# Two gate stages of an encoder trunk, ordered row by row at their end

## What is computed

```python
def encoder_trunk(x, p, W):
    h = x
    for i in range(DEPTH):                      # 2
        hn = rmsnorm(h, W['norm_mix_g'][i])
        h = h + mixer(hn)                       # attention (i = 0), gated delta rule (i = 1)
        h = h + expert_choice_moe(rmsnorm(h, W['norm_ffn_g'][i]), ...)
        gate = jax.nn.sigmoid(rmsnorm(h, W['norm_ple_g'][i]) @ W['ple_w_gate'][i])
        h = h + (p[i] @ W['ple_w_proj'][i]) * gate
    return rmsnorm(h, W['final_norm_g'])
```

## Time and profile before

| what | us |
|---|---|
| median of three runs | 1686.21 |
| the three runs | 1686.21, 1686.31, 1683.01 |
| span of the profiled execution (its own time is not listed apart) | 1680.5 |
| busy: TensorE, its weight loads, VectorE, ScalarE, GpSimd | 1587.1, 819.3, 675.9, 439.1, 203.6 |
| mean granted TensorE clock | 0.987 of 2.4 GHz |

### The profile page before, as it was taken

One profiled execution on the slowest core, in us unless ns is written; L12 is line 12 of the kernel. 1 busy time (PEld: TensorE's weight loads), 2 busy tenths in 40 slices (PEclk: granted clock), 3 DMA queues, 4 the chain that ended last, 5 costly groups with the idle time before them and its releaser, 6 DMA issues.

```text
span 1680.5 us, 21275 instructions
## 1 busy us (share of the span) xinstructions
PE 1587.1 (94%) x8960; PEld 819.3 (49%) x8960; DVE 675.9 (40%) x1130; ACT 439.1 (26%) x972; POOL 203.6 (12%) x120
## 2 busy tenths in 40 slices
PE   8999899999989988899999999998999999899887
PEld 4464534343343324588875688844344433433243
DVE  3564411131210216889983477684111302102056
ACT  4232301101101103422125776534011010110043
POOL 2302000000000004352402211220000000000031
PEclk9999999999999999999999999999999999999999
DMA  8104699999999995012121110276999999999941
GB/s 288 77 18 183 276 423 421 428 427 429 428 424 427 427 421 212 1 51 102 50 101 51 27 27 2 102 300 250 392 426 428 428 427 428 423 428 426 426 167 50
DMA packets 54045, 454.56 MB, mean 270 GB/s; under 512 B 5187, under 2 KB 7519, under 8 KB 28991
## 3 DMA queue, kind: packets, MB, share of 16 engines
q1 hardware_dynamic: 53424, 452.90, 65.6%
q0 software_dynamic: 288, 0.22, 0.0%
q10 hardware_dynamic: 239, 0.09, 0.0%
HBM read 451.07 MB, written 2.13 MB: 270 GB/s over the span
## 4 chain that ended last, share of the span: by engine, by line
PE 70%; DVE 12%; DMA 8%; ACT 6%; issue 3%; ACTq 0%; SPq 0%; DVEq 0%
PE banks L2154 34%; PE banks L1499 12%; DMA ring<-in_moe_w_down 4%; DMA ring<-in_p_sample 4%; DVE misc L2578 4%; PE banks L1682 3%; PE banks L2187 3%; PE banks L2125 3%; PE banks L1780 3%; PE banks L1745 2%; PE banks L2215 2%; PE banks L2163 1%; PE banks L1607 1%; DVE xn L2780 1%; DVE misc L2576 1%
## 5 line engine op out<-in xcount | busy, mean ns | idle before, releaser
L2154 PE MATMUL banks<-ring,misc 128*64 128x512 f32 x1952 | 433.8, 596 | 8.5 <-DMA ring<-in_moe_w_gate 4.4
L2154 PEld LDWEIGHTS banks<-ring,misc 128*64 128x64 f32 x1952 | 136.6, 137 | 276.3 <-issue 262.4
L2154 PE MATMUL banks<-ring,hid_t 128*64 128x512 f32 x960 | 216.0, 602 | 3.6 <-DMA ring<-in_moe_w_down 3.6
L3002 DVE TENSOR_TENSOR work<-work,banks 128x512 f32<-128x512 f32 x32 | 33.7, 1053 | 435.7 <-PE banks L2154 435.7
L1438 ACT ACTIVATE misc<-banks 32x512 f32<-32x512 f32 x64 | 37.6, 587 | 413.5 <-PE banks L2154 413.2
L2154 PEld LDWEIGHTS banks<-ring,hid_t 128*64 128x64 f32 x960 | 68.0, 139 | 141.8 <-issue 135.8
L3017 DVE COPY misc<-banks 32x512 f32<-32x512 f32 x64 | 44.2, 691 | 217.3 <-PE banks L2154 216.8
L819 POOL TENSOR_TENSOR ring<-ring 128x2048 f32<-128x2048 f32 x2 | 10.9, 5452 | 988.4 <-DVE ring L3053 988.4
L1499 PE MATMUL banks<-ring,xt 128*128 128x512 f32 (+1 forms) x280 | 118.9, 584 | 0.2
L2578 DVE SCALAR_TENSOR_TENSOR misc<-ring,conv_w,misc 128x512 f32<-128x512 f32 x96 | 93.8, 977 | 3.4
L1682 PE MATMUL banks<-ring 128*128 128x256 f32 x384 | 86.0, 380 | 0.0
(11 more groups left out here) (393 smaller groups left out, 1948.5 us busy)
## 6 DMA issues: line engine op xcount, KB each, us to landing
ring<-in_moe_w_up SPq DMA_DIRECT2D x62, 2048.0 KB, 19.1
ring<-in_moe_w_gate SPq DMA_DIRECT2D x60, 2048.0 KB, 17.6
ring<-in_moe_w_down SPq DMA_DIRECT2D x56, 2048.0 KB, 17.3
ring<-in_gdn_w_in SPq DMA_DIRECT2D x8, 2048.0 KB, 8.8
h<-in_moe_w_gate SPq DMA_DIRECT2D x4, 2048.0 KB, 16.2
ring<-in_ple_w_gate SPq DMA_DIRECT2D x4, 2048.0 KB, 12.0
ring<-in_moe_w_down SPq DMA_DIRECT2D x6, 1024.0 KB, 23.3
ring<-in_mla_w_out SPq DMA_DIRECT2D x2, 2048.0 KB, 24.3
```

What stands on the lines that cost most here:

```text
L2154: mm = pe.matmul(psum[64 * f:64 * f + 64, bank, :], tokens(4 * kh + k), row(k, f), start=(kh == 0 and k == 0), stop=(kh == 1 and k == 3))
L3002: dve.tensor_tensor(hid.rearrange("p (k q) -> p q k", k=4), sg.rearrange("p (q k) -> p q k", k=4), psum[:, 2 * (ex % 2) + 1, :].rearrange( ...
```

## The change

The change does four things. The last four products are issued as P7 t=0, P4 t=0, P7 t=1, P4 t=1, with a numbering of its own (`pg_no`) for the stage. On ScalarE the roots of rows 0 and 1 come ahead of `sigmoid(2, 1)`, and the rest goes row by row: (2, 1), (2, 0), (3, 1), (3, 0). On VectorE the norms of rows 0 and 1 come ahead of both P7s, and each row of the second sequence is finished from P7 and P4 in turn. In the final norm, the second half of row 3 is multiplied by its gain on VectorE ahead of time and scaled on ScalarE, VectorE does the first half, and the last output DMA waits for both.

```diff
+PG_ORDER = [(x, t) for x in (P1, P2, P6, P5, P3) for t in range(2)] + [(P7, 0), (P4, 0), (P7, 1), (P4, 1)]
+
+def pg_no(x, t):
+    return PG_ORDER.index((x, t))
...
-        PLE_ORDER = ((0, 0), (1, 0), (0, 1), (1, 1), (2, 1), (3, 1), (2, 0), (3, 0))
+        PLE_ORDER = ((0, 0), (1, 0), (0, 1), (1, 1), (2, 1), (2, 0), (3, 1), (3, 0))
...
-                sp.wait_ge(out_ready, j + 1)
+                sp.wait_ge(out_ready, j + 1 if j < NJ - 1 else NJ + 1)
                 sp.dma_start(y[0, (j % NT) * P:(j % NT + 1) * P, :], xn[:, j, :]).then_inc(out_done, 16)
...
             square(1, 1)
-            sigmoid(2, 1)
             act.activation(half_ss[:, 2 * NJ:2 * NJ + 1], eps[:, :], ACT.Sqrt)
             root(0, 5)
             root(1, 6)
             scaled(0)
             scaled(1)
-            sigmoid(3, 1)
+            sigmoid(2, 1)
             with_eps(2, 1, 10)
             sigmoid(2, 0)
-            with_eps(3, 1, 12)
             square(2, 0)
+            sigmoid(3, 1)
+            with_eps(3, 1, 13)
             sigmoid(3, 0)
             act.activation(half_ss[:, 2 * NJ:2 * NJ + 1], eps[:, :], ACT.Sqrt)
-            root(2, 13)
+            root(2, 11)
             square(3, 0)
             root(3, 15)
             scaled(2)
             scaled(3)
+            if name == "last":
+                act.wait_ge(rstd_done, NJ * norm_no[name] + NJ)
+                act.wait_ge(lb_done, 2)
+                act.activation(xn[:, NJ - 1, HALF:D], xn[:, NJ - 1, HALF:D], ACT.Copy, scale=rstd[:, NJ - 1:NJ]).then_inc(out_ready, 1)
...
-                gate_product(P7, a21, b12)
-                gate_product(P4, a22, b21)
+                gate_product(P7, a21, b12, (0,))
+                gate_product(P4, a22, b21, (0,))
+                gate_product(P7, a21, b12, (1,))
+                gate_product(P4, a22, b21, (1,))
...
-                    dve.scalar_tensor_tensor(out=xn[:, j, :], in0=h[:, j, :], scalar=rstd[:, j:j + 1], in1=fg,
+                    w = D if j < NJ - 1 else HALF
+                    dve.scalar_tensor_tensor(out=xn[:, j, 0:w], in0=h[:, j, 0:w], scalar=rstd[:, j:j + 1], in1=fg[:, 0:w],
...
                 for t in range(NT):
+                    dve.wait_ge(ple_added, 8 * l + 3 + t)
+                    norm(normed, t)
+
+                def second_half(t):
+
                     gate_add(pg_w[:, t, :], pg_w[:, t, :], P7, t, False)
                     gate_add(pg_q[:, t, :], pg_q[:, t, :], P7, t)
-                    dve.wait_ge(ple_added, 8 * l + 3 + t)
-                    norm(normed, t)
-                for t in range(NT):
-                    gated_add(NT + t, 1)
-                    if t == 0:
-                        dve.wait_ge(*L.s_pg.freed(out_no(P7, 1)))
-                        gate_add(pg_q[:, 0, :], pg_q[:, 0, :], P4, 0)
+
+                def first_half(t):
+
+                    dve.wait_ge(*L.s_pg.freed(pg_no(P7, t)))
+                    gate_add(pg_q[:, t, :], pg_q[:, t, :], P4, t)
+
+                second_half(0)
+                gated_add(NT, 1)
+                first_half(0)
+                second_half(1)
                 gated_add(NT, 0)
-                gate_add(pg_q[:, 1, :], pg_q[:, 1, :], P4, 1)
+                gated_add(NT + 1, 1)
+                first_half(1)
+                if l == 1:
+                    dve.wait_ge(ple_added, 8 * l + 7)
+                    dve.tensor_tensor(xn[:, NJ - 1, HALF:D], h[:, NJ - 1, HALF:D], fg[:, HALF:D], ALU.mult).then_inc(lb_done, 1)
                 gated_add(NT + 1, 0)
                 for t in range(NT):
-                    dve.wait_ge(ple_added, 8 * l + 7 + t)
+                    dve.wait_ge(ple_added, 8 * l + 6 + 2 * t)
                     norm(normed, NT + t)
```

More of the change, by code:

```diff
@@ L284, in ple_part @@
         def ple_part(j, f):
-            return out_no((P3 if f else P2) if j < NT else (P7 if f else P4), j % NT)
+            return pg_no((P3 if f else P2) if j < NT else (P7 if f else P4), j % NT)
         def pg_t(l):
@@ L568, in trunk_kernel @@
         conv_done, silu_q, sq16 = (sem(x) for x in ("conv_done", "qkv_silu", "head_squares"))
-        sums_done, kfac_done, lb_done = sem("sums_done"), sem("k_factors"), sem("beta_log")
+        sums_done, kfac_done, lb_done = sem("sums_done"), sem("k_factors"), sem("beta_log_and_final_gain")
         ba_exp, ba_dve, fac_done = sem("ba_exp"), sem("ba_dve"), sem("factors")
@@ L823, in ple_pool @@
                 pool.wait_ge(mo_weights, PLE_WEIGHTS[l] + 3)
-                pool.wait_ge(*lay[l].s_pg.full(out_no(P2, 1) + 1))
+                pool.wait_ge(*lay[l].s_pg.full(pg_no(P2, 1) + 1))
                 pool.tensor_tensor(b21, b21, t2, ALU.subtract).then_inc(mo_weights, 1)
@@ L1450, in _ @@
                 for t in range(NT):
-                    copy_out(L.s_pg, out_no(P1, t), pg_p1[:, t, :])
+                    copy_out(L.s_pg, pg_no(P1, t), pg_p1[:, t, :])
                 def sigmoid(j, f):
@@ L2274, in _, with gate_product @@
                 (t1, t2), (s1, s2) = pg_t(l), pg_s(l)
-                def gate_product(x, tokens, weights):
-                    for t in range(NT):
-                        product(L.s_pg, out_no(x, t), lambda k: tokens[:, k, t * P:(t + 1) * P], lambda k: weights[:, k, :], 4, HALF,
+                def gate_product(x, tokens, weights, ts=range(NT)):
+                    for t in ts:
+                        product(L.s_pg, pg_no(x, t), lambda k: tokens[:, k, t * P:(t + 1) * P], lambda k: weights[:, k, :], 4, HALF,
                                 L.s_pxt if x == P1 and t == 0 else None)
@@ L3032, in gate_add @@
                 def gate_add(out, src, x, t, last=True):
-                    i = out_no(x, t)
+                    i = pg_no(x, t)
                     dve.wait_ge(*L.s_pg.full(i + 1))
@@ L3056, in _ @@
                 for t in range(NT):
-                    dve.wait_ge(*L.s_pg.freed(out_no(P1, t)))
+                    dve.wait_ge(*L.s_pg.freed(pg_no(P1, t)))
                     gate_add(pg_c11[:, t, :], pg_p1[:, t, :], P2, t)
                 dve.wait_ge(mo_tokens, PLE_TOKENS[l] + 3)
-                L.s_pg.wait_read(dve, out_no(P2, 1))
+                L.s_pg.wait_read(dve, pg_no(P2, 1))
                 dve.tensor_tensor(a12, a12, s2, ALU.subtract).then_inc(mo_tokens, 1)
@@ L3066, in _ @@
                 for t in range(NT):
-                    dve.wait_ge(*L.s_pg.freed(out_no(P6, t)))
+                    dve.wait_ge(*L.s_pg.freed(pg_no(P6, t)))
                     gate_add(pg_w[:, t, :], pg_q[:, t, :], P5, t)
                 for t in range(NT):
-                    dve.wait_ge(*L.s_pg.freed(out_no(P5, t)))
+                    dve.wait_ge(*L.s_pg.freed(pg_no(P5, t)))
                     gate_add(pg_c12[:, t, :], pg_w[:, t, :], P3, t)
@@ L3075, in _ @@
                 for t in range(NT):
+                    dve.wait_ge(ple_added, 8 * l + 3 + t)
+                    norm(normed, t)
+                def second_half(t):
                     gate_add(pg_w[:, t, :], pg_w[:, t, :], P7, t, False)
                     gate_add(pg_q[:, t, :], pg_q[:, t, :], P7, t)
-                    dve.wait_ge(ple_added, 8 * l + 3 + t)
-                    norm(normed, t)
-                for t in range(NT):
-                    gated_add(NT + t, 1)
-                    if t == 0:
-                        dve.wait_ge(*L.s_pg.freed(out_no(P7, 1)))
-                        gate_add(pg_q[:, 0, :], pg_q[:, 0, :], P4, 0)
-                gated_add(NT, 0)
-                gate_add(pg_q[:, 1, :], pg_q[:, 1, :], P4, 1)
+                def first_half(t):
[5 more added lines that the diff above has]
+                second_half(1)
+                gated_add(NT, 0)
+                gated_add(NT + 1, 1)
[3 more added lines that the diff above has]
+                    dve.tensor_tensor(xn[:, NJ - 1, HALF:D], h[:, NJ - 1, HALF:D], fg[:, HALF:D], ALU.mult).then_inc(lb_done, 1)
                 gated_add(NT + 1, 0)
                 for t in range(NT):
-                    dve.wait_ge(ple_added, 8 * l + 7 + t)
+                    dve.wait_ge(ple_added, 8 * l + 6 + 2 * t)
                     norm(normed, NT + t)
```

## The result

The changed kernel takes 1689.12 us (median of 15 runs, 1686.53 to 1694.10), the kernel before 1685.58 (15 runs, 1681.51 to 1689.06). The ratio is 1.0025, 95% interval 1.0017 to 1.0033: slower by 0.25%, 4.2 us with 2.9 to 5.6. The profiled execution took 1687.37 us with a span of 1685.6.

A forecast was written before the change was run, and what follows sets the result against it. From P7 on, both gate stages were taken as a relay of VectorE and ScalarE; +2.44 us (first stage) and +1.8 (second stage and end) gave +4.2 on the median 1686.2, thus 1690.4 us, range 1685.5 to 1693.5.

The forecast's parts named there:

- Part 1, the early load: Gate stages: the first square-root table load starts earlier, by 1.09 us in the first layer and 1.82 in the second.
- Part 2, P7 behind the norms: VectorE, gate stages: row 0's P7 additions cost 1.20 us; idle before multiplication (2,1) 1.09 (first layer), 0.79 (second).
- Part 3, the order of the sigmoids: ScalarE, gate stages: sigmoid(3,1) behind square(2,0) leaves VectorE idle 1.39 us; sigmoid(3,0) comes 0.33 later.
- The later sigmoid(3,0): End of gate stages: behind square(3,1) and epsilon, it starts 1.07 us after P4's sum, 0.33 more than before.
- The products' order: TensorE's last four gate products: the new order itself costs and gives nothing.
- Part 4, the last half row: Final norm: row 3 gains 0.57 us, its transfer queues behind row 2's; second stage and end together +1.8 us.
- Rival (a), the clock: TensorE's turns at the high clock (-1.2 us) or shorter hand-overs (-0.6): sum 2.4 to 3.3, 1688.6 to 1689.5; chance 0.25.
- the smaller hand-overs: Small steps between instructions and engines are shorter than assumed: -0.6 us.
- Rival (b): Gate stages: sigmoids ready when asked for, so idle 2.48 and 2.18 us go; 1685.8, no change; chance 0.08.
- Rival (c): Gate stages: root wait covers P7's additions, sigmoids in time; gains 1.09, 1.82 and the half row's 0.57; 1682.7 us; chance 0.07.
- Rival (d): First layer: sigmoid table load holds ScalarE longer than its row, 1.28 us more; sum 5.5, 1691.7; chance 0.02.

The follow-up runs named there:

- experiment 2: Changed kernel with P7's two additions of row 0 ahead of both norms on VectorE: stages 26.42 and 24.33 us, changed kernel 26.41 and 26.17.
- experiment 1: Changed kernel with sigmoid(3,1) ahead of square(2,0) on ScalarE: stages 25.01 and 24.79 us, changed kernel 26.41 and 26.17.
- experiment 4: Changed kernel with TensorE's last four products in the old order (P7, P7, P4, P4): stages 26.41 and 26.18 us, changed kernel 26.41 and 26.17.
- experiment 5: Half row removed from the changed kernel: end 7.67 us, changed 7.58; half row alone put into the kernel before: end 7.59, before 7.72.
- experiment 6: Kernel before with only the early roots, P7 of row 0 ahead of both norms: stages 23.50 and 22.45 us, kernel before 23.98 and 24.26.
- experiment 3: Changed kernel with P7 of row 0 ahead of the norms and sigmoid(3,1) ahead of square(2,0): stages 25.02 and 22.93 us, changed 26.41 and 26.17.

## Why the prediction was right, point by point

The forecast was +4.2 us; the ratio says +4.2 (2.9 to 5.6), the medians +3.5, and the two stages and the end of the profiled executions +2.43, +1.91 and -0.14, together +4.2. The absolute 1690.4 stands 1.3 above the measured 1689.12. Some 0.6 of that is the kernel before, whose median over 15 runs is 1685.58 and not 1686.21.

- **Part 1, the early load.** Forecast 1.82 and 1.09 earlier, measured 1.83 and 1.11.
- **Part 2, P7 behind the norms.** Forecast 1.20 and an idle 0.79 in the second stage; measured together 2.0, by which VectorE comes sooner to P4 of row 0 in experiment 2; the row shows 0.69 as idle, because the idle time is counted from the end of the instruction before. The stage gets back 1.84 of it, since VectorE then meets TensorE's fifth product. For the first stage I had written 1.20 and 1.09 as two terms of a sum. The sum is right, the reading is not: experiment 2 takes the 1.20 away and gains nothing. There the limit is the table load behind the scaled rows, which the working had at 694.80 and counted as only 0.30 late (measured 694.35 in the changed kernel, which is 0.44 earlier in the span). P7's 1.20 and the idle 1.09 trade one for the other: with P7 ahead the idle time is 2.23.
- **Part 3, the order of the sigmoids.** Forecast 1.39 for sigmoid(3,1), measured 1.38 and 1.40 by experiment 1; the row shows 1.31 of it as idle. The later sigmoid(3,0): forecast 1.07 from P4's start, measured 1677.39 - 1676.32 = 1.07. Sums forecast +2.44 and +1.90, measured +2.43 and +1.91.
- **The products' order** was costed at nothing; experiment 4 shows it.
- **Part 4, the last half row.** ScalarE's half row took the 0.72 forecast (the first stage of the kernel before has a row of that length, a scaled half row of L972 at 693.25), VectorE's 0.75 and not 0.69, which costs 0.03. Forecast for the end from the second load: 7.6 (1682.3 less 1674.7), measured 7.58; the queueing is shown by experiment 5.
- **Rival (a), the clock.** It came in part and gave nothing. The stretch from 709.5 to 710.0 has a granted clock of 0.53, so it came back at about 709.97, 32.5 us after the start of the 48 records. Before it was 709.92, 32.0 us. The work came 2.43 later, the clock only 0.5. That is one execution: in the ten profiled executions the clock came back between 30.5 and 35.5 us after the records, and in the other two kernels with the changed order 33.1 and 33.5. (The prediction has the fall of the clock before at 703.3; the 0.59 of its row puts it at 703.1, which changes nothing.) So the turns' second part ran partly at the high level:

```profile
708.95 1.54 PE L1480 MATMUL banks<-ident,xn 128*128 128x128 f32 x8
...
717.52 0.33 PE L1528 MATMUL banks<-ident,work 128*128 128x128 f32 x1 [1.04 <-DVE work L2339]
```

  VectorE still started to empty the turned rows 5.72 us after the load, as before, and TensorE later waited for it 1.04 us, before 0.60. The bound of -1.2 can be approached, though. In the profiled execution of experiment 6 the clock was still high when the turns began (stretch, TensorE busy with count, granted clock):

```profile
706.00:707.00 1.00, 0.97 (x8) 0.94 0.00 0
```

  Eight turns took 1.20 us in place of 1.97, and VectorE started 4.95 us after the load, 0.77 earlier. This is outside the two measures of the table and in none of its gains. The rival's sum of 2.4 to 3.3 does not follow from its two terms: the smaller hand-overs alone (-0.6) give 3.6, above the 3.4 that it was to stay under.
- **Rival (b)**, ScalarE holds nobody up: excluded by the waits for sigmoids in the rows of the result and by experiment 1. **Rival (c)**, faster: its condition, P7 inside the wait and the sigmoids in time, is experiment 6 nearly to the letter, and there the kernel is 2.3 us faster in its stages, not the 2.9 of the two roots, for the first stage keeps only 0.48 of its 1.09. The half row's 0.57, the rest of the rival's 3.5, brings about 0.1 by experiment 5. **Rival (d)**, a load longer than its row: in ScalarE's rows of experiment 2 the load of 695.17 ends at 696.45 and the sigmoid starts at 696.47. The Trainium skill (ScalarE: Activation LUTs, "What ACT_TABLE_LOAD costs") adds about 1380 ns of drain to every switch; no such time is in this row, and the sums of both stages leave no room for it.

One step of the forecast was weaker than it looked: it set three times, 2.5 to 5.8 us above the span of the profiled execution, beside that span, as if they belonged together. Executions of which both are known have 1.7 to 1.8 between span and time (1685.6 and 1687.37). By that the profiled execution of before took about 1682.3 and was a quick one of its scatter. The median came out because the difference was added to the median, not to the span; that the median of three, 1686.21, stood within 0.6 of the one of fifteen was in part luck, for the three alone reach down to 1683.01.

## What to carry to other kernels

When two in-order engines hand work to each other, an order that finishes one item at a time makes every hand-over a wait; the old order interleaved two rows and hid each engine behind the other's work on the other row. Write the two queues out side by side with start times before moving anything: twenty steps from one trace gave both stages within 0.02 us. What a single step is worth is another matter: the 1.20 of P7 was right in the sum of the first stage, and taking it away there gained nothing. And ask of each waiting instruction that is moved what was filling its wait, and of a last transfer that is to start earlier whether the one ahead of it has left.

## What the runs showed of the hardware

The executions scatter more than the change is worth, and in parts that it does not touch. Between VectorE's first emptying of the turned rows and TensorE's 48 products of the second layer's mixer, nine of ten profiled executions lie between 406.4 and 406.8 us; the changed kernel's was 407.77. In its stretches (us, TensorE busy with count, granted clock, DMA share, GB/s) the clock goes to the low level for some 3 us:

```profile
1095.00:1096.00 1.00, 0.54 (x4) 0.84 0.00 0
1096.00:1097.00 1.00, 1.00 (x6) 0.50 0.00 0
1097.00:1098.00 1.00, 1.00 (x7) 0.50 0.00 0
1098.00:1099.00 1.00, 1.00 (x7) 0.50 0.00 0
1099.00:1100.00 1.00, 1.00 (x10) 0.95 0.00 0
```

TensorE had waited 1.88 us for VectorE just before, and its next 16 turns took 3.51 us. In the kernel before it waited 1.90 at the same place and the turns took 1.96; in all eight kernels of the experiments they took 1.96 to 1.97 after 1.71 to 1.94 of waiting. The kernel of experiment 5 that has the whole change but the half row has the same code there as the changed one, and its middle, from TensorE's turn behind the first stage to the second stage's records, took 942.95 us, where before took 943.32 and the changed kernel 944.66. So this is scatter and no effect of the change, and it is 1.1 of the 1.34 us by which the two spans differ in the middle. From those 48 products to the second gate stage, mostly the second layer's experts (DMA share 0.98 from 1150 to 1600 us), it took between 533.6 and 536.6 us, with the same code in every kernel; what makes that scatter was not looked for.

So a single span misleads: for the kernel of experiment 3 it is 1682.7, 2.2 us above the kernel before, while its two stages and its end together are 0.4 us shorter (+1.04, -1.33, -0.09). A change of a few us in a kernel of this length is read from the stretch that it touches, and the times of many runs only confirm the sum.
